# A two-block fp32 network on one core: FFN gate and up pairs as seven products of block sums, with gated values kept in HBM

## The reference

```python
h = rmsnorm(x, norm_ffn_g[l])
g = dwconv(jnp.einsum("bsd,df->bsf", h, w_gate[l]), conv_ffn_w[l])   # 1024 -> 2816, 3 taps
v = jnp.einsum("bsd,df->bsf", h, w_up[l])
x = x + jnp.einsum("bsf,fd->bsd", jax.nn.silu(g) * v, w_down[l])
...
shift, scale, gate = jnp.split(c_act @ ada_w[l] + ada_b[l], 3, axis=-1)   # the "ada" rows
```

## Time and profile before

| | |
|---|---|
| median of 3 runs | 2056.44 us (2055.55 to 2057.53) |
| profiled execution, span from the first to the last instruction | 2054.3 us |
| FFN blocks 1 to 21 and all output jobs | some 347 to 1045 us of the span |
| instructions | 24800 |

### The profile page before, as it was taken

One profiled execution on the slowest core, in us unless ns is written; L12 is line 12 of the kernel. 1 busy time (PEld: TensorE's weight loads), 2 busy tenths in 40 slices (PEclk: granted clock), 3 DMA queues, 4 the chain that ended last, 5 costly groups with the idle time before them and its releaser, 6 DMA issues.

```text
span 2054.3 us, 24800 instructions
## 1 busy us (share of the span) xinstructions
PE 2040.3 (99%) x9324; PEld 1677.7 (82%) x9324; DVE 1208.7 (59%) x1701; ACT 662.9 (32%) x1154; POOL 768.7 (37%) x474
## 2 busy tenths in 40 slices
PE   9999999999999999999999999999999999999998
PEld 7888888888888888888888888888888878777887
DVE  6999677555644555455665544355355381397556
ACT  6323345121122221221264122122122162498112
POOL 4677726222222222122167122132132174265633
PEclk9999999999999999999999999999999999999999
DMA  4231112322233213232102112121021112010202
GB/s 158 72 113 41 52 42 92 123 102 92 71 103 121 102 51 112 102 115 105 47 21 72 41 52 62 31 57 55 31 62 51 31 42 67 11 28 25 63 20 82
DMA packets 44828, 139.93 MB, mean 68 GB/s; under 512 B 5696, under 2 KB 10960, under 8 KB 44752
## 3 DMA queue, kind: packets, MB, share of 16 engines
q1 hardware_dynamic: 32736, 100.68, 15.7%
q10 hardware_dynamic: 12016, 38.23, 5.0%
HBM read 134.67 MB, written 7.36 MB: 69 GB/s over the span
## 4 chain that ended last, share of the span: by engine, by line
PE 92%; ACT 3%; POOL 2%; DVE 2%; issue 1%; DMA 0%; SPq 0%; POOLq 0%; DVEq 0%; ACTq 0%
PE psum L669 28%; PE psum L671 27%; PE psum L670 27%; POOL temp L506 2%; PE psum L736 1%; PE psum L737 1%; PE psum L738 1%; ACT probs L1544 1%; PE psum L1036 1%; PE psum L1020 1%; PE psum L1008 1%; PE psum L795 1%; PE psum L797 1%; PE psum L796 1%; ACT w_hi L1538 1%
## 5 line engine op out<-in xcount | busy, mean ns | idle before, releaser
L471 POOL TENSOR_TENSOR w_lo<-w_raw,w_hi 128x1024 fp32r<-128x1024 f32 x174 | 442.2, 2557 | 969.3 <-ACT w_hi L1136 964.1
L669 PE MATMUL psum<-norm_hi,w_hi 128*128 128x512 f32 (+1 forms) x1648 | 639.1, 388 | 0.0
L670 PE MATMUL psum<-norm_lo,w_hi 128*128 128x512 f32 (+1 forms) x1648 | 637.7, 387 | 0.0
L671 PE MATMUL psum<-norm_hi,w_lo 128*128 128x512 f32 (+1 forms) x1648 | 637.7, 387 | 0.0
L669 PEld LDWEIGHTS psum<-norm_hi,w_hi 128*128 128x128 f32 x1648 | 309.5, 188 | 63.4 <-issue 0.2
L670 PEld LDWEIGHTS psum<-norm_lo,w_hi 128*128 128x128 f32 x1648 | 309.5, 188 | 62.9 <-issue 0.2
L671 PEld LDWEIGHTS psum<-norm_hi,w_lo 128*128 128x128 f32 x1648 | 309.5, 188 | 62.8
L1678 DVE SCALAR_TENSOR_TENSOR stream<-psum,mods,stream 128x512 f32<-128x512 f32 x160 | 119.7, 750 | 170.5 <-PE psum L671 170.4
L1207 ACT ACTIVATE temp<-psum 128x512 f32<-128x512 f32 x160 | 93.3, 598 | 390.5 <-PE psum L671 366.7
L1136 ACT CAST w_hi<-w_raw 128x1024 fp32r<-128x1024 f32 x157 | 158.3, 1046 | 148.3 <-PE psum L671 79.6
L1676 DVE TENSOR_TENSOR stream<-psum,stream 128x512 f32<-128x512 f32 x176 | 118.7, 689 | 83.9 <-PE psum L671 83.7
(11 more groups left out here) (225 smaller groups left out, 2934.8 us busy)
## 6 DMA issues: line engine op xcount, KB each, us to landing
w_raw<-in_slabs SPq DMA_DIRECT2D x175, 512.0 KB, 3.5
ada_raw<-in_ada ACTq DMA_DIRECT2D x10, 3072.0 KB, 12.7
stream<-in_x SPq DMA_DIRECT2D x8, 512.0 KB, 9.5
skew_scratch<-row_scratch ACTq DMA_DIRECT2D x1, 3072.0 KB, 17.3
ada_raw<-in_ada ACTq DMA_DIRECT2D x1, 2048.0 KB, 8.0
out<-stream SPq DMA_DIRECT2D x4, 512.0 KB, 2.8
out<-stream SPq DMA_DIRECT2D x7, 256.0 KB, 2.2
bias<-skew_scratch ACTq DMA_DIRECT2D x4, 192.0 KB, 3.7
```

What stands on the lines that cost most here:

```text
L471: nc.gpsimd.tensor_tensor(WL[place][:, :], RAW[at % 2][:, :], WH[place][:, :].bitcast(f32), ALU.subtract).then_inc(slab_ready, 1)
L669: nc.tensor.matmul(dst, wh, xh, start=n == 0, stop=False)
L670: nc.tensor.matmul(dst, wh, xl, start=False, stop=False)
L671: last = nc.tensor.matmul(dst, wl, xh, start=False, stop=n == len(terms) - 1)
```

## The change

Twenty of the 22 pairs (blocks 2 to 21; `SEVENS`) no longer use eight block products. Gate and up weights are read as a 2 x 2 block matrix (gate or up, low or high input channels), the normed stream as another (low or high channels, first or second half of the tokens). Seven products of sums of these blocks (`seven_products`), of 12 matmuls each, are combined by additions into the four tiles. For this:

- The sums of the stream's blocks are made once, ahead of the first seven (POOL: four corner sums; DVE: `corner_sums`; ACT: `corner_cast`; DVE and POOL the lows). One of them overwrites a corner of `HH` and `HL`, for which the second pair does its second half of tokens first.
- The sums of the weights' blocks are made for each pair on POOL (`weight_sums`, four of 512), cast by ACT (`gate_cast`, `s1_cast`, `s2_cast`, `s34_cast`) and lowered by POOL (`gate_low`, `sum_lows`, `last_low_of`).
- ACT copies three of the seven results from their banks (`keep_part`, four copies), DVE adds the others (six additions of 512), POOL one sum (`mixed_part_sum`).
- The first tap moves from DVE to ACT (`first_tap`) for blocks 2 to 21.
- The gated values of blocks 2 to 19 go to HBM as they are (`keep_y`, 0.5 MB each) and come back in the output phase, where ACT and DVE split them (`back_cast`, `back_low`).
- All 11 output jobs follow in a phase of their own (`JOBS`). The stream `X` is stored to HBM meanwhile (4 MB out, 4 MB back); its room holds a second pair of raw and gate buffers (`EVEN_RAW`, `EVEN_GATE`) and the `ada` rows, now four a turn in turns 1 to 16.

The core of the diff (turn `n` handles the products of block `n + 2`; `t` is the count of tiles at its start):

```diff
+            def weight_sums(n):
+                raw = seven_raw(n)
+                a11, a12, a21, a22 = raw[0][:, hs(0)], raw[0][:, hs(1)], raw[1][:, hs(0)], raw[1][:, hs(1)]
...
+                nc.gpsimd.tensor_tensor(a11, a11, a21, ALU.subtract).then_inc(sums_made, 1)
+                gp.wait_ge(sums_made, 4 * n + 1)
+                nc.gpsimd.tensor_tensor(a21, a21, a22, ALU.add).then_inc(sums_made, 1)
+                gp.wait_ge(tiles, seven_tile(n - 1) + 4 if n else FFN_TILE + 4)
...
+                nc.gpsimd.tensor_tensor(s2, a22, a11, ALU.subtract).then_inc(sums_made, 1)
+                gp.wait_ge(sums_made, 4 * n + 3)
+                nc.gpsimd.tensor_tensor(a12, a12, s2, ALU.subtract).then_inc(sums_made, 1)
...
+            for n in range(SEVENS):
+                last_low_of(n)
+                if n + 1 < SEVENS:
+                    gate_low(n + 1)
+                    weight_sums(n + 1)
+                mixed_part_sum(n)
+                if n + 1 < SEVENS:
+                    sum_lows(n + 1)
+            lows(ROW_SLAB, POOL_SLAB)
...
+            def seven_products(n):
+
+                gate = seven_gate(n)
+                pe.wait_ge(gate_lo, n + 1)
+                pe.wait_ge(*((part_kept, 4 * n - 2) if n else (act_read, 45)))
+                product(bank[0], gate[0], gate[1], 0, *plain_part(0, 0))
+                pe.wait_ge(*((part_added, 6 * n - 5) if n else (act_read, 46)))
+                product(bank[1], gate[0], gate[1], 512, *plain_part(1, 0))
+                pe.wait_ge(s1_lo, n + 1)
+                pe.wait_ge(*((part_added, 6 * n) if n else (act_read, 47)))
...
+                product(bank[2], WH[2], WL[2], 0, *plain_part(0, 1))
+                pe.wait_ge(s2_lo, n + 1)
+                pe.wait_ge(*((part_added, 6 * n - 4) if n else (act_read, 48)))
...
+                product(bank[3], WH[4], WL[4], 0, *extra_part(0))
...
+                product(bank[4], WH[2], WL[2], 512, *extra_part(2))
+                pe.wait_ge(s34_lo, n + 1)
...
+                product(bank[5], WH[3], WL[3], 512, *plain_part(1, 1))
+                pe.wait_ge(part_kept, 4 * n + 3)
...
+                product(bank[2], WH[3], WL[3], 0, *extra_part(1))
```

ACT and DVE in a turn, in order (casts, taps and additions as above):

```diff
+            for n in range(SEVENS):
+                t = seven_tile(n)
+                last = n == SEVENS - 1
+                if n:
+                    s34_cast(n)
+                gate_silu(n + 1)
+                for half in range(2):
+                    keep_part(t + 1, body(T[0], half), bank[0])
...
+                    gate_cast(n + 1)
+                act.wait_ge(f_mul, n + 2)
+                keep_part(t + 3, body(T[1], 1), bank[2])
+                if not last:
+                    s2_cast(n + 1)
+                keep_part(t + 5, body(T[1], 0), bank[4])
...
+                    s1_cast(n + 1)
+                    if n < ADA_TURNS:
+                        load_ada(n)
+                first_tap(n)
...
+                gate_times_up(n + 1)
...
+                add(body(T[0], 0), bank[1], body(T[0], 0), [(tiles, t + 2), (part_kept, 4 * n + 1)])
...
+                    ada_rows(n - 1, range(2))
+                add(body(T[0], 1), bank[3], body(T[0], 1), [(tiles, t + 4), (part_kept, 4 * n + 2)])
+                add(body(T[1], 1), body(T[0], 1), body(T[1], 1), [(part_added, 6 * n + 2), (part_kept, 4 * n + 3)])
+                if ada:
+                    ada_rows(n - 1, range(2, ADA_ROWS))
+                    ada_store(n - 1)
...
+                add(body(T[0], 1), bank[5], body(T[1], 1), [(tiles, t + 6), (part_added, 6 * n + 3), (part_mixed, n + 1)])
+                gate_conv(n + 2)
+                add(body(T[1], 1), bank[2], body(T[1], 1), [(tiles, t + 7)])
+                add(body(T[1], 0), bank[2], body(T[1], 0))
```

The start, on DVE and on ACT:

```diff
+            corner_sums(0)
+            dve.wait_ge(act_read, 44)
+            gate_conv(0)
+            corner_sums(1)
+            gate_times_up(0)
+            y_low(0)
+            t1_low(0, 4)
+            t1_low(1, 5)
...
+            y_cast(0)
+            act.wait_ge(tiles, FFN_TILE + 6)
+            corner_cast(1, 0)
+            corner_cast(1, 1)
+            corner_cast(2, 1)
+            corner_cast(4, 1)
+            corner_cast(3, 1)
+            for j, (T_n, half) in enumerate(((0, 1), (1, 1), (0, 0), (1, 0))):
+                act.wait_ge(*((f_mul, 1) if T_n else (f_conv, 1)))
+                read_tile((FFN_TILE + 4 + j, j), body(T[T_n], half))
```

More of the change, by code:

```diff
@@ L86, in slab_ends @@
         down()
-    products(2)
-    for _ in range(FFN_LOOPS - 1):
-        products(2), products(2), down()
-    products(2), products(2), products(2, False), down(), down()
+    products(2), products(2)
+    t += 7 * SEVENS
+    for _ in JOBS:
+        down()
     for _ in range(GROUPS):
@@ new lines, in product, with plain_part @@
+            def product(dst, wh, wl, at, xh, xl):
+                for k in range(4):
+                    cols = slice(at + P * k, at + P * k + P)
+                    nc.tensor.matmul(dst, wh[:, cols], xh(k), start=k == 0, stop=False)
+                    nc.tensor.matmul(dst, wh[:, cols], xl(k), start=False, stop=False)
+                    last = nc.tensor.matmul(dst, wl[:, cols], xh(k), start=False, stop=k == 3)
+                last.then_inc(tiles, 1)
+            def plain_part(low_rows, half):
+                return (lambda k: HH[:, 4 * low_rows + k, hs(half)]), (lambda k: HL[:, 4 * low_rows + k, hs(half)])
@@ new lines, in _ @@
+                    if last and j == STAT_AT[POOL] + 1:
+                        spread(POOL, 0)
+                    if n == 0 and j < 4:
+                        pe.wait_ge(*((part_kept, 4 * SEVENS - 2) if j == 0 else (part_added, 6 * SEVENS - (6, 5, 4, 2)[j])))
+                    else:
+                        pe.wait_ge(dve_read, d + j - 3)
+                    cols = slice(P * e, P * e + P)
+                    products(down_bank(j), [(WH[place][:, cols], WL[place][:, cols], yh[:, hs(half)], yl[:, hs(half)])
+                                            for place, (yh, yl) in zip(JOB_PLACES[n], ys)]).then_inc(tiles, 1)
@@ L1358, in _ @@
+            gate_cast(0)
             act.wait_ge(c_loaded, 16)
[L1359 to L1374 removed]
@@ new lines, in add_rows @@
+            def add_rows(n, behind=None):
+                dve.wait_ge(dve_read, 64 + 16 * n)
+                for j in range(16):
+                    half, e = divmod(j, 8)
+                    if n == 0 and e == 0:
+                        dve.wait_ge(x_back[half], 16)
+                    dve.wait_ge(tiles, DOWN_TILE + 16 * n + j + 1)
+                    part = X[:, e, hs(half)]
+                    nc.vector.tensor_tensor(part, down_bank(j), part, ALU.add).then_inc(dve_read, 1)
+                    if behind:
+                        behind(j)
@@ L1976, in _ @@
+            add_rows(0, last_y)
+            for n in range(1, len(JOBS) - 1):
+                add_rows(n, lambda j: back_low(n + 1, (j - 3) // 3) if j in (3, 6) else None)
+            dve.wait_ge(gains_done, 4)
+            add_rows(len(JOBS) - 1, lambda j: apply_early(POOL, j))
             apply(POOL, 16 - STAT_AT[POOL])
```

610 lines of the change are left out of this document (422 added, 188 removed).

## The result

The changed kernel takes 2045.43 us (median of 4 runs, 2045.0 to 2046.22) against 2056.07 for the kernel before (4 runs). The ratio is 0.9949, 95% interval 0.9934 to 0.9963: faster by 0.5%, where 2080.5 was forecast. The profiled execution has a span of 2043.5 us, against 2054.3: -10.8, where the sum had +24.1.

What follows compares the result with a forecast made beforehand. PE's matmuls were taken to bound the kernel before. Terms: -54.4 (240 matmuls fewer), +58.8 (turns), +18.2 (start), +1.5 (loop's end) = +24.1, forecast 2080.5 us, range 2066 to 2101 holding about 0.8.

Steps and rivals of the forecast that it cites:

- a loop: Each turn (one loop round, seven products): closed chain over ACT, POOL and DVE, 17.3 us without DVE's two-SBUF operations, 22.5 with.
- The end of the loop: Last turn: the first output product waits for both row slabs' lows, +1.5 us, between 0 and 4.
- The `ada` load: Rival, turns 1 to 16: the `ada` rows arrive 2.9 us late, turns near 25.3, +45, 2126 us; chance 0.08.
- the deciding point: Length of a turn from which downwards the change was said to win: 21.1 us.
- the price of the port in a turn: Four `ada` products and one 512-wide sum alternate with POOL's operations, adding 5.3 us: turns of 22.5 against PE's 19.04.
- The 0.68 us sum: DVE's 512-wide sum of two SBUF halves in each turn, charged 0.68 us for taking turns with POOL.
- The number of turns: Turns 1 to 17 were each charged 22.5 - 19.04 us, +58.8 in all.
- The start: Before the first of the seven products, PE waits for ACT's read of bank 0: +18.2 us, bounds 13 to 24.
- The output phase: The phase of output jobs after the loop: expected to cost nothing; up to 10 us if its cover fails.
- The port is full but the order yields: Rival: turns take only the port's total time, 20.2 to 20.5 us, giving 2045 us; chance 0.05.
- Port waits do not show: Rival: DVE rows run at 1.2 us beside POOL, turns take PE's 19.04, -48, 2008 us; chance 0.07.
- The clock falls in the wait: Rival: PE's clock drops behind each turn's wait, 7.5 us a turn, +127, 2208 us; chance 0.03.

Runs made afterwards that it cites:

- experiment 1: Changed kernel, with the four `ada` products of each turn taking their second operand from PSUM instead of SBUF: 2017.5 us, ratio 0.9812.
- experiment 3: Changed kernel with one of three matmuls per step of the seven products left out: 2041.87 us; the same with `ada` products' second operand from PSUM: 1985.75.
- experiment 2: Changed kernel, with only the first of each turn's four `ada` products taking its second operand from PSUM: 2031.29 us, ratio 0.9881.
- experiment 8: Changed kernel, with DVE's twelve corner-sum operations taking their second operand from free PSUM banks instead of SBUF: 2030.94 us, ratio 0.9878.
- Experiment 5: Changed kernel with the bias added once, 64 wide, at the end: 2045.58 us; with ACT's next gate cast also moved ahead of the silu: 2018.26 us.
- second kernel of experiment 3: Changed kernel with one of three matmuls per step of the seven products left out and `ada` products' second operand from PSUM: 1985.75 us.
- Experiment 6: Changed kernel with the start reordered: DVE multiplies the first tile earlier, ACT reads the second pair's tiles ahead of five casts: 2050.31 us, ratio 0.9972.
- two edits: On the changed kernel: ACT's next gate cast ahead of the silu (2044.5 us alone), one bias addition at the end (2045.58 alone); together 2018.26.

## Why the prediction was wrong, step by step

*Right.* There are 240 matmuls fewer at 0.2267 us (PE's busy time fell by 50.3; the slow stretch takes part of it back). The mechanism is right: two-SBUF operations of DVE and POOL's take turns, and this closes a loop; PE waits at its third product for DVE's last addition, in 16 turns and in none of the last two. There is one wait at the start, released by ACT's read of bank 0. The end of the loop was 1.5 and is 1.5. The `ada` load is not late: DVE's products never stood idle for it (the 0.0 at the end of their row in experiment 1). And the deciding point holds: a turn of 21.1 us was named as the one from which the change wins; it is 20.81, and it wins.

*The step that failed* is the price of the port in a turn, "4 x 1.145 + 0.68 = 5.3 us, less 0.1: 22.5 us". Measured, the four products cost 3.63 us (experiment 3; 0.87 for the first alone, experiment 2), 0.85 less than their share. The 0.68 us sum costs 0.33, since the POOL operation behind it takes 1.58 from start to start, and 1.26 where it is alone (experiment 3): 0.35 less. The third part is in the bare links of the loop. Spans plus handings-over gave 17.3; the measured 17.17 still holds the sum's 0.33, so the bare links are 16.8, 0.5 less. Together these are the 1.7 us between 22.5 and 20.8.

A blocked operation's span holds its wait, and DVE's spans in these rows run up to 0.1 us into the next, so spans added up come out long. What a clash costs is the delay of the next start. The rows before had it: POOL's pair grew from 4.76 to 5.73 us, 0.97, with one product between its two operations. The sum took 1.145 from another row. The bounds varied the handings-over only (22.0 to 23.1) and left the price of a clash out. With 0.87 to 0.97 for each product the turn would have come out at 21.4 to 21.8, and the sum at +5 to +12, still too long by the 512-wide sum and the bare links.

*The number of turns.* 17 were charged, 16 waited. Turn 1 goes free here: its third product starts at 410.43, 26.3 us behind the first product of all, 1.8 of them for slow matmuls. In experiment 8, which has no slow matmuls at the start, the same distance is 26.0 (369.75 to 395.79), with a wait of 1.4 in it. So the 1.8 us of slow pitch stand in the place of a 17th wait.

*The start* was 18.2; the wait is 14.4, and with the slow pitch 16.2. 0.5 of the difference is a misread row: 347.40 is when ACT starts to read, the second pair starts at 347.88. The stated bound of 13 would also be 5.2 below 18.2, where the range took 4.

*What was missing.* The output phase was put at nothing; it gave 2.5, of which 2.4 are the changes between pairs and jobs that the kernel before had.

*The rivals.* "The port is full but the order yields" had 2045, which is the time that was measured, but not for its reason: the loop was closed as forecast, POOL idle 1.82 us in each turn. That the number agrees is chance. Experiment 5 shows what that rival describes, and it comes to TensorE's pace there, 2018, so the port's own 20.2 us a turn was too high as well. "Port waits do not show" falls with experiments 1 and 8. "The clock falls in the wait": between 347 and 1040 us it fell once, in the 14.3 us at the start, and not behind any of the 16 waits of 1.5 us (granted clock 1.00 from 431 to 743 us). The rule of the Trainium skill named there ("TensorE: Matmul & The Clock Gate", section "HAM oscillation — how this bites in real kernels") is borne out where the waits are longer: in the second kernel of experiment 3 the clock is 0.50 behind a wait of 4.3 us (445.6 to 449.0) and 1.00 behind one of 1.5 (462.7 to 466.0).

*As a sum it was weak in another way.* Start and turns were added. Experiment 6 shows that, while the turns are held by the chain, the start counts by when the chain begins: there PE started earlier and the kernel ended later.

## What to carry to other kernels

Where two engines take turns at a port, price a clash by how much later the next operation starts beside one, from start to start in the trace, and put the spread of that price into the range; whole spans and handings-over counted together come out too long. Before cutting a closed chain, look for the next one: two edits worth 1 us and nothing alone were worth 27 us together. And a small operation with two SBUF inputs is not small when it is queued behind a long one on the other engine and something late stands behind it.

## What was not expected of the hardware

- An addition of 128x4 elements took 1.13 us beside POOL's 512-wide sums and 2.23 us beside its 1024-wide low; with nothing of POOL's to wait for, 0.16 to 0.24 us (experiment 3, second kernel).
- The `ada` product (multiply and sum in one, fp32) is shut out like an addition when both inputs lie in SBUF, 2.31 us in the mean, and not at all with one in PSUM, 1.21.
- Among short waits close together (3.6, 2.8 and 1.8 us within 25 us) 26 matmuls ran at the slow pitch; behind a single one of 14.2 us it was 9.
